# RWKV: the products of the inverses and of the masked matrix with V, 64 columns in place of 128

## What is computed

```python
def step(state, inp):
    r_t, d_t, k_t, v_t, kk_t, a_t = inp
    sa = jnp.einsum('bhij,bhj->bhi', state, -kk_t)
    state = (state * d_t[:, :, None, :] + sa[..., None] * (kk_t * a_t)[:, :, None, :]
             + v_t[..., None] * k_t[:, :, None, :])
    return state, jnp.einsum('bhij,bhj->bhi', state, r_t)
```

## Time and profile before

| | us |
|---|---|
| median of 3 runs | 2937.23 |
| lowest and highest | 2936.66, 2939.68 |
| profiled execution, its time | 2938.9 |
| profiled execution, its span | 2937.1 |
| TensorE busy in it | 2777.1 (95%) |
| weight loads busy | 2190.7 (75%) |
| VectorE, ScalarE, GpSimd busy | 1286.8, 1121.8, 127.8 |
| mean granted TensorE clock | 0.978 of full |

### The profile page before, as it was taken

How to read it: one execution, slowest core, us unless ns; L and a number is a source line. 1 busy time by engine, 2 the same in 40 slices (tenths; PEclk the granted TensorE clock), 3 DMA queues, 4 the chain that set the end, 5 groups by cost and what they waited for, 6 DMA issues and landing times.

```text
span 2937.1 us, 44160 instructions
## 1 busy us (share of the span) xinstructions
PE 2777.1 (95%) x18364; PEld 2190.7 (75%) x18364; DVE 1286.8 (44%) x2139; ACT 1121.8 (38%) x2023; POOL 127.8 (4%) x129
## 2 busy tenths in 40 slices
PE   8989889999999999999999999999899999999998
PEld 6879657887877887878797666666598876666665
DVE  5456257545547744665465122221286451122212
ACT  5454236445446422364453222222364342222222
POOL 0000000000000121200010000000001300000000
PEclk9999889999999999999999999999999999999999
DMA  8524657545435211064344899999742048999996
GB/s 333 200 103 173 263 223 271 204 170 213 176 127 192 96 58 58 30 229 183 118 174 170 334 418 417 415 416 417 321 146 85 1 158 330 416 417 413 418 415 256
DMA packets 96403, 701.55 MB, mean 239 GB/s; under 512 B 10688, under 2 KB 10816, under 8 KB 11328
## 3 DMA queue, kind: packets, MB, share of 16 engines
q1 hardware_dynamic: 96192, 698.59, 59.9%
HBM read 697.50 MB, written 1.05 MB: 238 GB/s over the span
## 4 chain that ended last, share of the span: by engine, by line
PE 89%; DVE 5%; ACT 3%; issue 2%; DMA 1%; SPq 0%; DVEq 0%; ACTq 0%
PE bank L1589 15%; PE bank L826 12%; PE bank L828 12%; PE bank L827 12%; PE bank L1649 8%; PE bank L1567 4%; PE bank L1676 4%; PE bank L1927 2%; PE bank L1935 2%; PE bank L1939 2%; PE bank L2601 1%; PE bank L1458 1%; PE bank L1461 1%; PE bank L1473 1%; DMA weight_ring<-weight_slots 1%
## 5 line engine op out<-in xcount | busy, mean ns | idle before, releaser
L1589 PE MATMUL bank<-weight_ring,packed_h 128*64 128x256 f32 x2176 | 285.4, 379 | 0.0
L826 PE MATMUL bank<-source_hi_lo,weight_hi_lo 128*128 128x256 f32 x864 | 252.2, 292 | 12.7 <-DVE source_hi_lo L816 8.9
L1589 PE MATMUL bank<-more_slots,packed_h 128*64 128x256 f32 x1920 | 257.0, 379 | 1.5 <-ACT packed_h L1576 1.5
L826 PE MATMUL bank<-gate_up_hi_lo,x_hi_lo 128*128 128x512 f32 x640 | 253.2, 396 | 1.4 <-DVE gate_up_hi_lo L944 1.4
L1589 PEld LDWEIGHTS bank<-weight_ring,packed_h 128*64 128x64 f32 x2176 | 196.4, 137 | 74.3 <-issue 18.1
L828 PE MATMUL bank<-gate_up_hi_lo,x_hi_lo 128*128 128x512 f32 x640 | 249.8, 390 | 0.0
L827 PE MATMUL bank<-gate_up_hi_lo,x_hi_lo 128*128 128x512 f32 x640 | 249.3, 390 | 0.0
L827 PE MATMUL bank<-source_hi_lo,weight_hi_lo 128*128 128x256 f32 x864 | 247.0, 286 | 0.0
L828 PE MATMUL bank<-source_hi_lo,weight_hi_lo 128*128 128x256 f32 x864 | 246.7, 286 | 0.0
L1589 PEld LDWEIGHTS bank<-more_slots,packed_h 128*64 128x64 f32 x1920 | 174.0, 137 | 69.7 <-issue 15.4
L785 DVE TENSOR_TENSOR weight_hi_lo<-weight_ring,weight_hi_lo 128x1024 fp32r<-128x1024 f32 x141 | 171.8, 1222 | 87.6 <-ACT weight_hi_lo L779 87.3
(11 more groups left out here) (569 smaller groups left out, 5329.4 us busy)
## 6 DMA issues: line engine op xcount, KB each, us to landing
weight_ring<-weight_slots SPq DMA_DIRECT2D x443, 1024.0 KB, 7.5
more_slots<-weight_slots SPq DMA_DIRECT2D x212, 1024.0 KB, 9.1
params_sb<-small_params SPq DMA_DIRECT2D x1, 3196.5 KB, 18.6
h_sb<-weight_slots SPq DMA_DIRECT2D x3, 1024.0 KB, 5.9
y_sb<-weight_slots SPq DMA_DIRECT2D x3, 1024.0 KB, 8.0
x_sb<-x_by_tokens SPq DMA_DIRECT2D x1, 1024.0 KB, 4.8
out_by_tokens<-x_sb SPq DMA_DIRECT2D x4, 256.0 KB, 2.2
params_sb<-small_params SPq DMA_DIRECT2D x1, 70.5 KB, 4.6
```

The source lines that it names most:

```text
L826: e.matmul(out, w[0], x[0], start=start, stop=False, skip_group_check=shared)
L1589: mm = e.matmul(ps[x * CAP:(x + 1) * CAP, m * FB:(m + 1) * FB], self.hc[:, c, (2 * (p % 2) + x) * CAP:(2 * (p % 2) + x + 1) * CAP], wt[:, ...
```

## The change

A product of `par` is made only for the 64 columns that belong to `par`: `f` cuts both what streams (V_tokens, LakV or W) and where the result goes in the bank. The other 64 columns of the bank are not written; they were not read before either. `heads4(ps)` is the bank's view as 128 x 4 x 128.

```diff
             if par == 0:
                 e.wait_ge(*k.ge("tokens", n, it, "V"))
+            f = slice(par * 64, par * 64 + 64)
             for m in range(4):
-                mm = e.matmul(ps[:, m * P:(m + 1) * P], self.bufs[par]["nl"][:, m, :], self.tok["V"][:, m, :], start=True, stop=True)
+                mm = e.matmul(heads4(ps)[:, m, f], self.bufs[par]["nl"][:, m, :], self.tok["V"][:, m, f], start=True, stop=True)
             mm.then_inc(*k.up("lak_v", n, it, par))
...
                 e.wait_ge(*k.ge(*inv[par].done()))
+                f = slice(par * 64, par * 64 + 64)
                 for m in range(4):
-                    mm = e.matmul(ps[:, m * P:(m + 1) * P], self.bufs[par]["tt"][:, m, :], (self.W if j else self.lv)[:, m, :], start=True, stop=True)
+                    mm = e.matmul(heads4(ps)[:, m, f], self.bufs[par]["tt"][:, m, :], (self.W if j else self.lv)[:, m, f], start=True, stop=True)
                 mm.then_inc(*k.up("U_product", n, it, j, par))
```

## The result

The changed kernel takes 2945.2 us (median of 8 runs, 2944.2 to 2949.8), the kernel before 2936.6 (8 runs, 2932.1 to 2939.7). The ratio is 1.0033 with a 95% interval of 1.0022 to 1.0044: slower by 6 to 13 us. The profiled execution took 2945.2 us with a span of 2943.4, where that of before took 2938.9 and 2937.1.

A forecast was written before the change was run, and what follows sets the result against it. TensorE was taken to bound the kernel. Pitch 0, group ends -0.6 and clock +7.7 gave +7.1 us: 2944.3 us by the median of 2937.2, range 2935.5 to 2950.

The forecast's parts named there:

- part (a): U and lv products: time from one pass to the next stays 0.111 us, set by weight loads; 0 us.
- Rival 2: U and lv products: streamed columns set the time between passes, so 9.5 us less, 2927.7 us; chance 0.04.
- part (b): Last load to consumer, second U groups and first lv groups: 0.05 us less at each of 12, 0.6 us saved.
- part (c): Chain of states, U steps: TensorE's clock falls to half in 5 more stretches of 1.53 us, 7.7 us lost.
- more of the line's matmuls above 400 ns: Sign at the U products' line: more matmuls would last above 400 ns if the clock fell more often.
- The prediction's price: Cost of one low stretch, from W's start to the second U_half: 4.37 us against 2.84, 1.53 us more.
- rival 3: Chain of states: low stretches hang together, one prolonging the next, 8 and more; 2948.8 us or beyond; chance 0.10.
- The granted clock of the stage: Sign in the RWKV stage, 998 to 1250 us: granted clock at 0.93 to 0.97, where it was 0.99.
- Rival 1: TensorE's clock stays as it is, leaving only the earlier group ends: 2936.6 us, no change; chance 0.33.

The follow-up runs named there:

- the two kernels whose clock is full: Kernel before and changed kernel, each with 256-column products in the chain of states' waits and 512-column ones at later stage starts: 2929.9 and 2929.6 us.
- the two fills: Changed kernel plus overwritten products where TensorE is about to wait in the chain of states: one of 256 columns, 2933.1 us, or two of 4, 2948.9 us.
- The narrow fill: Changed kernel plus two overwritten products of 4 columns at each place in the chain of states where TensorE is about to wait: 2948.9 us, again 2948.6.
- the wide one: Changed kernel plus one overwritten product of 256 columns at each place in the chain of states where TensorE is about to wait: 2933.1 us.
- 96 columns: Changed kernel with lv and U streaming 96 columns, the 64 needed and 32 beside them: 2937.0 us, 0.9997 of the kernel before.
- each stage start: Changed kernel with the 256-column products in waits, plus four products of 512 columns at the start of every stage but the first: 2929.6 us.

## Why the prediction was right, step by step

- **The pitch, part (a), 0 us.** Right: 1.86 us for 16 loads, at 64 columns as at 128. The rows of another stage with the same shape carried over. Rival 2 is out. One row didn't fit a price by loaded columns alone: half of 0.111 would be 0.056 us for a load of 64x64, and the earlier trace rows show 0.033. Nothing of the sum rests on it.
- **The end of a group, part (b), -0.6 us.** Right in mechanism and size: 0.05 us at one group, and 235.4 - 234.8 = 0.6 us over the stage between the two kernels whose clock is full.
- **The clock, part (c), +7.7 us.** Right in mechanism: shown by the two fills, which differ in what they stream and hardly in busy time, and by the stage time that follows the time at half clock. The size was the product of a guessed count and a price read from one step, and that it came out this close is luck. Five further stretches of 3.4 us were taken; 23.8 - 6.8 = 17.0 us, five times 3.4, came in the first profile, 20.4 in the second. Each was priced at 1.53 us; measured are (6.4 + 0.6) / 5 = 1.40.
- **Where.** Here the prediction was off. It put the low stretches on the U steps. The first and the last of the changed kernel, from 1110.8 and 1244.0 us, lie on the y products behind a U step, the third on state and gate products; only the second, from 1175.7, takes in the end of a U step. The U step is where less streams, and what comes next pays. So one sign of the prediction, more of the line's matmuls above 400 ns, failed: there are 2 of 128 where there were 27, and the U products are busy 16.09 us in place of 19.21 (windows of the line alone, after and then before):

```profile
...
1001.00:1250.00 249.00, 16.09 (x128) 15.11 (x128) 0.95 0.11 43
...
```

```profile
...
1001.00:1250.00 249.00, 19.21 (x128) 17.65 (x128) 0.99 0.11 43
...
```

The prediction's price, from a U step, was carried over to other products; measured on y it is 2.69 / 2 = 1.35 us. And three of the four lasted 6.8 us, one following the other, which the prediction had only in rival 3.
- **Sum.** +7.1 us were forecast and 8.6 measured between the medians (2945.2 - 2936.6), 6.3 between the profiled executions. The granted clock of the stage was expected at 0.93 to 0.97 and is 0.95.
- **The rivals.** Rival 1 had rested on the doubt that the narrow stretch of the earlier trace rows was also a small part of the array. The narrow fill has a full 128x128 load, and it does not hold the clock where the wide one does. The Trainium skill (TensorE: Matmul & The Clock Gate, Part 1) says that activity releases the throttle of the clock. The fills agree only in part: with nearly the same busy time (241.6 and 242.3 of 252 us) one kernel had 30.6 us at half clock and the other none.

What stays open: why 96 columns cost nothing that can be measured, and why one kernel with the same instructions has 6.8 us at half clock in one execution and 30.6 in another. That the falls depend on how the waits and the products lie in time isn't shown; one or two profiles for each kernel don't settle it. Also open is how much each stage start gave.

## What to carry to other kernels

Before narrowing a product, look whether the weight load sets the pitch (here 0.111 us with 128 and with 64 columns behind a load of 128x128): if so, what streams is free, and cutting it gains only the end of each group (0.05 us here). Where TensorE goes back and forth with other engines, those free columns may be what keeps its clock at 2.4 GHz; look at the granted clock of the stretch before and after, and at low stretches already there. And a wide product in a wait, into a bank that is overwritten anyway, can be worth more than the columns that were cut: here 12 us off the changed kernel, in a chain in which nothing else was changed. It won back what the cut had lost; in the kernel before, the same fills gained nothing that can be measured.

## What the runs showed of the hardware

- Wide products (256 columns) placed in the waits took the stage from 23.8 us at half clock to none; products of 4 columns with nearly the same busy time had 30.6 in a usual execution, and 6.8 in their quickest.
- One and the same kernel differs between executions by which stretches run at half clock: with the narrow fill 2934.1 us at a mean clock of 0.981 and 2953.4 at 0.971. A single profile can be of either kind: 6.8 and 30.6 us at half clock in the stage.
- A stretch at half clock in the chain of states costs 1.3 to 1.5 us for 3.4 us: (244.1 - 234.8) / 7 = 1.33 between the changed kernel and the one with the wide fill (23.8 us at half clock are seven times 3.4), which includes what the fills cost.
